# Down rows of two FFNs as pairs of seven half-width products, with part of their sums added by transfers

## The reference

```python
def swiglu(x, w_gu, w_down):
    g, u = jnp.split(x @ w_gu, 2, axis=-1)
    return (jax.nn.silu(g) * u) @ w_down
...
x = x + 0.5 * swiglu(rmsnorm(x, norm_ffn1_g[l]), ffn1_w_gu[l], ffn1_w_down[l])
...
x = x + 0.5 * swiglu(rmsnorm(x, norm_ffn2_g[l]), ffn2_w_gu[l], ffn2_w_down[l])
```

## Time and profile before

| | us |
|---|---|
| median of 3 runs | 1753.06 (1752.43 to 1754.81) |
| the profiled execution | 1753.69 |
| its span | 1751.5 |
| TensorE busy | 1745.0 (100%) |
| VectorE busy | 1180.3 (67%) |
| ScalarE busy | 847.4 (48%) |
| GpSimd busy | 135.4 (8%) |

### The profile page before, as it was taken

One profiled execution on the slowest core, in us unless ns is written; L12 is line 12 of the kernel. 1 busy time (PEld: TensorE's weight loads), 2 busy tenths in 40 slices (PEclk: granted clock), 3 DMA queues, 4 the chain that ended last, 5 costly groups with the idle time before them and its releaser, 6 DMA issues.

```text
span 1751.5 us, 26596 instructions
## 1 busy us (share of the span) xinstructions
PE 1745.0 (100%) x10407; PEld 1535.1 (88%) x10407; DVE 1180.3 (67%) x1843; ACT 847.4 (48%) x1442; POOL 135.4 (8%) x150
## 2 busy tenths in 40 slices
PE   9999999999999999999999999999999999999998
PEld 7889989878888899988888998988877888989897
DVE  7848748666776546865784784876688677747474
ACT  6425526454333335743553562654655543727274
POOL 0001011000000001100010110100232000000000
PEclk9999999999999999999999999999999999999999
DMA  5356556332123457733355655634421235555552
GB/s 184 89 166 176 145 151 151 111 106 85 53 85 107 114 151 177 175 108 98 95 149 140 168 150 150 173 100 131 141 61 61 85 96 138 127 145 141 142 139 72
DMA packets 92618, 220.65 MB, mean 126 GB/s; under 512 B 10800, under 2 KB 12080, under 8 KB 92496
## 3 DMA queue, kind: packets, MB, share of 16 engines
q1 hardware_dynamic: 74640, 186.29, 34.2%
q0 software_dynamic: 16576, 30.60, 10.8%
q10 hardware_dynamic: 1280, 2.08, 0.3%
HBM read 214.74 MB, written 2.10 MB: 124 GB/s over the span
## 4 chain that ended last, share of the span: by engine, by line
PE 97%; DVE 1%; ACT 0%; issue 0%; DMA 0%; DVEq 0%; ACTq 0%; POOLq 0%
PE ps L2083 19%; PE ps L2085 19%; PE ps L2084 19%; PE ps L2175 10%; PE ps L2177 10%; PE ps L2176 10%; PE ps L2105 2%; PE ps L2107 2%; PE ps L2106 2%; PE ps L2324 0%; PE ps L2454 0%; PE ps L2479 0%; PE ps L2465 0%; PE ps L2327 0%; PE ps L2312 0%
## 5 line engine op out<-in xcount | busy, mean ns | idle before, releaser
L2083 PE MATMUL ps<-Ahi,wh 128*128 128x512 f32 x913 | 357.1, 391 | 0.0
L2084 PE MATMUL ps<-Alo,wh 128*128 128x512 f32 x913 | 355.3, 389 | 0.0
L2085 PE MATMUL ps<-Ahi,wl 128*128 128x512 f32 x913 | 355.3, 389 | 0.0
L2175 PE MATMUL ps<-BThi,wh 128*128 128x256 f32 x1232 | 340.5, 276 | 0.0
L2176 PE MATMUL ps<-BTlo,wh 128*128 128x256 f32 x1232 | 340.4, 276 | 0.0
L2177 PE MATMUL ps<-BThi,wl 128*128 128x256 f32 x1232 | 340.4, 276 | 0.0
L571 ACT ACTIVATE wh<-raw 128x1024 fp32r<-128x1024 f32 (+1 forms) x206 | 213.1, 1036 | 222.3 <-PE ps L2085 187.9
L1189 DVE TENSOR_TENSOR wl<-raw,wh 128x1024 fp32r<-128x1024 f32 (+1 forms) x206 | 250.2, 1215 | 64.7 <-ACT wh L571 62.7
L2176 PEld LDWEIGHTS ps<-BTlo,wh 128*128 128x128 f32 x1232 | 231.6, 188 | 0.0
L2175 PEld LDWEIGHTS ps<-BThi,wh 128*128 128x128 f32 x1232 | 231.3, 188 | 0.0
L2177 PEld LDWEIGHTS ps<-BThi,wl 128*128 128x128 f32 x1232 | 231.3, 188 | 0.0
(11 more groups left out here) (367 smaller groups left out, 2729.0 us busy)
## 6 DMA issues: line engine op xcount, KB each, us to landing
raw<-in_w_gu SPq DMA_DIRECT2D x96, 256.0 KB, 3.7
raw<-in_w_d SPq DMA_DIRECT2D x32, 512.0 KB, 3.6
raw<-in_w_dn SPq DMA_DIRECT2D x32, 512.0 KB, 3.9
raw<-in_w_gu SPq DMA_DIRECT2D x22, 512.0 KB, 3.6
raw<-in_w_up SPq DMA_DIRECT2D x36, 256.0 KB, 3.8
sa<-in_w_gu SPq DMA_DIRECT2D x32, 256.0 KB, 3.8
sa<-in_w_gu POOLq DMA_DIRECT2D x32, 256.0 KB, 4.9
sc<-in_w_gu SPq DMA_DIRECT2D x32, 256.0 KB, 3.9
```

The source lines that it names most:

```text
L2083: pe.matmul(ps, wh[:, c], hi[:, k, :], start=(k == 0), stop=False)
L2084: pe.matmul(ps, wh[:, c], lo[:, k, :], start=False, stop=False)
L2085: last = pe.matmul(ps, wl[:, c], hi[:, k, :], start=False, stop=(k == nb - 1))
L2175: pe.matmul(ps, whi[:, w], bhi, start=(new and kp == 0), stop=False, skip_group_check=not new)
```

## The change

In both FFNs of the first block, the down rows of the first two groups become pairs: `DQ` numbers them, four for each group. The third group's rows stay units.

- **Order** (`SEQ`): the up pair of the inner tile behind a group now stands ahead of the group's down pairs (ups to tile 8, four down pairs, ups 9 to 16, four down pairs, ups 17 to 21, eight down units).
- **Activations**: for inner tiles 0 to 15 the gated product is written straight into blocks of `BF` or a new `DF`, and `pair_a` and `a_lo` go. For every two inner tiles VectorE makes the sums (`t_sums`, three operations), ScalarE one copy of 128 × 1792 (`t_high`) and VectorE one subtraction of the same size (`t_low`) into seven operands `DThi`, `DTlo`, which lie over `Ahi`, `Alo`, `Hhi` and `Hlo`. In the pair stage these stand in the iteration after each odd inner tile (and, in FFN 1, `t_high` and `t_low` of tiles 4 and 5 in the first pair), in the unit stage in iterations 1 to 4.
- **Results**: four half-width operations of VectorE add half of a product to its quarter of `X` (`x_add`); they stand where `merge` and `product` stand in an up pair. ScalarE's three taps are scaled (`x_tap`) and kept in `TA[5]`, `TA[8]` and `TA[6]`; GpSimd's queue adds them to `X` by two accumulating transfers, 128 × 256 and 128 × 512 (`kept`).
- **GpSimd's queue**: `kept` of pair m-2 stands ahead of the two transfers of pair m.
- The rows of `w_d` lie in another order of inner tiles (even ones first) in memory; the scratch for GpSimd's descriptors is 4096 bytes in place of 8192.

```diff
+        ups(0, 9)
+        downs(0)
+        ups(9, 17)
+        downs(1)
+        ups(17, 22)
+        downs(2)
...
+        def kept(p):
+
+            k, q = UNITS[p][1], DQ[p]
+            pool.wait_ge(s["tp"], 3 * PAIR[p] + 3)
+            pool.wait_ge(s["ev"], EV0[p] + 3)
+            pool.dma_start(X[:, k + 1, RIGHT], TA[6][:, (LEFT, RIGHT)[q % 2]], accum_op=ALU.add).then_inc(s["dk"], 16)
+            pool.dma_start(X[:, k, :], TA[(5, 8)[q % 2]], accum_op=ALU.add).then_inc(s["dk"], 16)
+
         def added(pairs):
-            for p in pairs:
+            pairs = list(pairs)
+            for m, p in enumerate(pairs):
+                if m > 1 and pairs[m - 2] in DQ:
+                    kept(pairs[m - 2])
...
+            def t_high(g, kp):
+
+                act.wait_ge(s["ts"], 8 * f + 4 * g + kp + 1)
...
+                act.activation(DThi[kp][:, :, :], act_blocks(g, kp)[:, 0:NP, :], ACT.Copy).then_inc(s["th"], 1)
+
+            def x_tap(p, i):
...
+                if i == 0 and q > 1:
+                    act.wait_ge(s["dk"], 32 * q - 32)
+                act.wait_ge(s["pe"], PEN[p][c])
+                act.activation(dst, BK[BANK[p][b]][:, LEFT], ACT.Copy, scale=scale).then_inc(s["tp"], 1)
...
+                t(p, 1)
+                pair_next(v, 0)
+                t(p, 2)
+                if i == 0 and f == 0:
+                    t_high(0, 2)
+                elif last[0] == "up" and last[1] < 16 and last[1] % 2 == 1:
+                    t_high(last[1] // 8, last[1] % 8 // 2)
+                pair_next(v, 1)
...
+            def t_low(g, kp):
+                dve.wait_ge(s["th"], 8 * f + 4 * g + kp + 1)
+                dve.tensor_tensor(DTlo[kp][:, :, :], act_blocks(g, kp)[:, 0:NP, :], f32(DThi[kp][:, :, :]),
+                                  ALU.subtract).then_inc(s["tl"], 1)
+
+            def x_add(p, i):
+
+                k = UNITS[p][1]
+                if i == 0 and DQ[p] % 8 == 4 and k == 0:
+                    dve.wait_ge(s["dk"], 32 * DQ[p])
+                b, c, dst, scale = ((2, 3, X[:, k, LEFT], 0.5), (0, 4, X[:, k + 1, RIGHT], -0.5),
+                                    (1, 5, X[:, k, RIGHT], 0.5), (0, 6, X[:, k + 1, LEFT], -0.5))[i]
+                dve.wait_ge(s["pe"], PEN[p][c])
+                dve.scalar_tensor_tensor(out=dst, in0=BK[BANK[p][b]][:, LEFT], scalar=scale, in1=dst,
+                                         op0=ALU.mult, op1=ALU.add).then_inc(s["ev"], 1)
...
+                if last[0] == "up":
+                    product(last[2], last[1])
+                elif last[0] == "dn":
+                    x_add(last[2], 3)
+                pair_lo(p, 4)
...
+                if due:
+                    t_sums(*tile, 0)
+                pair_lo(p, 5)
+                if due:
+                    t_sums(*tile, 1)
+                pair_lo(p, 6)
+                if due:
+                    t_sums(*tile, 2)
+                if v in PAIR:
+                    pair_lo(v, 0)
+                    total(v, 0)
+                if kind == "up":
                     merge(p, 0, TA[2][:, LEFT])
+                else:
+                    x_add(p, 0)
...
+            product(UP[f, 21], 21)
+            dve.wait_ge(s["dk"], 256 * f + 256)
...
+            if p in DQ:
+                return DThi[kp][:, c, :], DTlo[kp][:, c, :]
...
+                    if p in DQ and c == 0 and UNITS[p][1] == 0:
+                        pe.wait_ge(s["tl"], 4 * (DQ[p] // 4) + kp + 1)
```

More of the change, by code:

```diff
@@ new lines, in ffn @@
+            for i, (kind, j, p) in enumerate(SEQ[f]):
+                v = p + 2
+                last = SEQ[f][i - 1] if i > 0 else (None, 0, 0)
+                t = tap if kind == "up" else x_tap
+                pair_hi(p, 4)
+                if kind == "up" and j > 16:
+                    pair_a(j - 1)
+                t(p, 0)
+                pair_hi(p, 5)
+                pair_hi(p, 6)
+                t(p, 1)
[7 more added lines that the diff above has]
+                if v in PAIR:
+                    pair_hi(v, 2)
+                    pair_hi(v, 3)
+                else:
+                    hi(v)
+                    hi(v + 1)
+                if kind == "up":
@@ new lines, in ffn @@
+            for j in range(JS[f]):
+                u = UP[f, j]
+                kp = j - JS[f] + 5
+                if f == 0 and j == 0:
+                    lo(3)
+                    lo(4)
+                    norm(1, 1, 5)
+                elif j == 0:
+                    lo(u + 2)
+                    sums_lo(5, SS[:, :], Ahi, Alo)
+                    norm(6, 3, u + 3)
+                times_r(u, TA[j % 2])
+                if kp > 0:
+                    low_blocks(2 * f, kp - 1)
+                elif kp == 0:
+                    normed(2 * f, kp)
+                if j in (2, 4):
+                    t_low(0, j // 2 - 1)
+                dve.wait_ge(s["silu"], f * FT + j + 1)
+                own.add(dve.tensor_tensor(TA[4 + j % 2], TA[2 + j % 2], R[:, :], ALU.mult))
+                if j == JS[f] - 1:
+                    total(u + 2, 0)
+                    pair_lo(u + 2, 2)
+                elif j > 0 and (f == 1 or j > 2):
+                    lo(u + 3)
+                if 0 < kp < 4:
+                    normed(2 * f, kp)
+                dve.wait_ge(s["pe"], PEN[u + 1])
+                tiles_free(j)
+                own.wait()
+                dve.tensor_tensor(halves(j), BK[BANK[u + 1]][:, :].rearrange("p (h t) -> p h t", h=2),
+                                  TA[4 + j % 2].rearrange("p (h t) -> p h t", h=2), ALU.mult).then_inc(s["ev"], 1)
+                if f == 0 and j < 3:
+                    lo(6 + j)
+                elif j < JS[f] - 2:
+                    lo(u + 4)
+                elif j == JS[f] - 2:
+                    pair_lo(u + 4, 0)
+                    pair_lo(u + 4, 1)
+                else:
+                    pair_lo(u + 2, 3)
+                if 0 <= kp < 4:
+                    sums_of_blocks(2 * f, kp)
+                if j % 2 == 1:
+                    for step in range(3):
+                        t_sums(0, j // 2, step)
+                if j == JS[f] - 1:
+                    total(u + 2, 1)
@@ L1415, in ffn @@
                     dve.wait_ge(s["ev"], EV0[p])
                     merge(p, 1, TA[1][:, RIGHT])
[L1417 to L1440 removed]
+                else:
+                    x_add(p, 1)
@@ new lines, in ffn @@
+                if i == 0 and f == 0:
+                    t_low(0, 2)
+                elif due:
+                    t_low(*tile)
+                if v in PAIR:
+                    pair_lo(v, 2)
+                else:
+                    lo(v)
+                if kind == "up":
+                    merge(p, 2, TA[2][:, RIGHT])
+                else:
+                    x_add(p, 2)
+                if v in PAIR:
+                    pair_lo(v, 3)
+                    total(v, 1)
+                else:
+                    lo(v + 1)
@@ new lines, in ffn @@
+            product(UP[f, 21], 21)
+            dve.wait_ge(s["dk"], 256 * f + 256)
+            for n in range(KT):
+                u = DN[f, 2] + n
+                if n == 0:
+                    a_lo(22 * f, 5, TA[4])
+                feed(u + 2)
+                dve.wait_ge(s["pe"], PEN[u])
+                dve.scalar_tensor_tensor(out=X[:, n, :], in0=BK[BANK[u]][:, :], scalar=0.5, in1=X[:, n, :],
+                                         op0=ALU.mult, op1=ALU.add).then_inc(s["ev"], 1)
+                if n > 0:
+                    sums(n - 1)
+                dve.wait_ge(s["ev"], EVN[u])
+                after(n)
@@ L2644, in _tiles, with _halves @@
     return np.ascontiguousarray(w.reshape(k // P, P, n // P, P).transpose(2, 1, 0, 3))
+def _halves(w, groups):
+    order = list(range(w.shape[2]))
+    for a, b in groups:
+        order[a:b] = list(range(a, b, 2)) + list(range(a + 1, b, 2))
+    return np.ascontiguousarray(w[:, :, order, :])
 def _wide(w):
```

370 lines of the change are left out of this document (165 added, 205 removed).

## The result

The changed kernel took 1800.49 us (median of 4 runs, 1797.34 to 1804.18) against 1752.86 for the kernel before (4 runs beside it): a ratio of 1.0271, 95% interval 1.0257 to 1.0285. The forecast was "slower", by 10 us; it is slower by 48, and the time lies above the range.

A forecast was written before the change was run, and what follows sets the result against it. The prediction took TensorE to bound the kernel, busy for the whole span. From 1753.7 us, −21.6 (TensorE) +2 (VectorE) +29.9 (loop through GpSimd's queue) gave 1764.0, against the median 1763.4; range 1757 to 1779.

The forecast's parts named there:

- the loop: GpSimd's queue: third `x_add` of pair m-2, kept transfers, `sa`, `total`, next third `x_add`; 7.5 us a group, +29.9 us.
- TensorE's part: In four groups, eight down rows at 43.5 us become four pairs at 9.52 each, 38.1: −21.6 us.
- VectorE's part: VectorE keeps up on average; lateness in heavy iterations and at the first down pair costs +2 us (0 to 8).
- about 1.3 and 0.6: Lateness in us in FFN 1, where two heavy iterations follow each other, then the first down pair.
- the unit stage ... nothing: `t_low` in unit iterations 2 and 4 fits, 10.8 us of VectorE in the 10.9 of two units: no cost.
- ScalarE's part: Copies and taps take 5.5 of 9.52 us a pair and two `t_high` are cheaper than four `pair_a`: no cost.
- Hand-overs: Some six passes between engines in one closed turn through GpSimd's queue, at 0.04 us each: 0.25 us.
- Issues: GpSimd issuing the two kept transfers ahead of `sa`, 0.86 us each: 1.7 us a turn.
- La: Time from issue to landing of `sa` behind two kept transfers: 6.6 us, ends 4.2 and 7.6.
- L: Length of one closed turn through GpSimd's queue and VectorE, 4.85 us plus the landing of `sa`: 11.45 us.
- Break-even: Point where waits through GpSimd's queue cost 19.6 us over four groups, with `sa` landing in 5.96 us.
- Rival A: In GpSimd's queue `sa` lands in time and the kernel is faster, 1733.5 us without a stall; chance 0.28.

The follow-up runs named there:

- the version without the loop: The changed kernel with both kept transfers of pair m-2 issued behind the two sum transfers of pair m, not ahead: 1751.54 us, 0.9991 of the kernel before.
- the 4.3 with nothing ahead: Median landing of `sa` in us in the changed kernel with only the kept transfers moved behind, their wait left ahead of `sa`: 1751.5 us.
- the tiny transfers: The changed kernel, same order and waits, with each kept transfer carrying 8 columns in place of 256 or 512: 1780.7 us, 1.0154 of the kernel before.

## Why the prediction was wrong

The sign and the place were right. Four things were wrong: the gain of TensorE was put too high, and the costs of VectorE, of the loop and of slower up pairs too low.

- **TensorE's part, −21.6.** The shape is that of the up pairs, the time is not: 10.08 us a down pair, not 9.52, so 16 × 0.56 = 9.0 us of the gain never came. The step that failed is "the matmuls have the shape of today's pairs", taken as "the same time". Moving operands and weights by 64 to 256 bytes showed that the place counts.
- **VectorE's part, +2 (0 to 8).** Measured 8.8 in the version without the loop, with the slower clock behind the wait of 2.6 us in FFN 2. Of the waits named in FFN 1 ("about 1.3 and 0.6") one is there, 1.1 us before product 7 of the second pair; the first down pair has none. The failed step is "the unit stage ... nothing": the sum of the amounts fits, but the last iteration holds `t_low` ahead of the sum for the first pair. It was moved, and 4.0 us came back. The rest stays; VectorE is busy for 20.9 of 23.2 us there, which may be why, and no run tested it.
- **ScalarE's part, 0.** Right as an amount; ScalarE only hands on the wait for `total`. SP's queue cost nothing either.
- **The loop, 4 × 7.5 = +29.9.** Measured 45.5. By its parts: VectorE 2.9 forecast, 2.90 measured. Hand-overs 0.25 forecast, 0.68 measured: 0.12 from the landing to `total`, but 0.56 from the end of `x_add` to GpSimd's queue; I had taken six at 0.04 between VectorE and ScalarE and none to GpSimd. Issues 2 × 0.86 = 1.7: the queue issues 0.54 apart (the row that I cited, four in 2.19 us, already has 0.55 each), but the durations grow by 0.36 each (0.87, 1.22, 1.58), so `sa` is through 2.65 us after the first starts where it would be through after 0.87 alone, 1.78 more. Of the landing of 7.90 from its start, 0.71 belong to that; what is left is **7.2 against La = 6.6**. The term in La that failed is the queueing behind the two kept transfers: I put at most 1.7 on a median of 4.9, with 1.7 read from two issues that stood 1.71 apart, which shows no rate of the queue; against the 4.3 with nothing ahead they add 2.9. Together L = 12.56, not 11.45: 16 × 1.11 = 17.8 us. Since twelve of the turns are measured against 10.08 and not 9.52, 6.7 fall off. That makes 29.9 + 17.8 − 6.7 = 41.0. Up to the start of product 7 of the up pair behind each group, where the last wait ends, the trace has 11.4, 10.0, 10.5 and 10.0, together 41.9. The other 3.6 are that product itself: 12 matmuls that take 1.36 us without the loop and 1.5, 2.7, 2.7 and 2.1 with it, in three of the groups at the half clock. The prediction had no term for the clock.
- **The rest.** More up pairs ran at 118 ns than before: 4.1 us in the version without the loop. The kernel before has such pairs too, at the start of FFN 2 (912.3 to 922.2 and 922.2 to 932.1, 9.89 us each at a full clock); the prediction took its period from FFN 1 alone. Behind the loop's groups, the up pairs from the second on lose 5.2 us more, about 3.4 by the half clock that goes on into the second one and 1.8 by more pairs at 118. Nothing in the prediction spoke of that.

The sum: −21.6 + 9.0 + 8.8 + 4.1 = +0.3 for the version without the loop (spans: −0.2), then + 45.5 + 5.2, less 0.9 for FFN 2's first pair, whose wait has no half clock behind it in the changed kernel: +50.1 (spans: 49.6). Break-even stands wrong too: even with no loss in the loop this change is worth 0.1% at most (0.9991, interval 0.9982 to 1.0001), not 1.1%.

Rival A asked whether `sa` lands in time. In the changed order it does not; with the kept transfers behind it does, and still the time is 1751.5 and not rival A's 1733.5, for the first two reasons of the list and the slower up pairs. The Trainium skill's fit for GpSimd's DMAs (DMA: Bandwidth & Descriptors, Anatomy of one DMA — SWDGE (gpsimd) path), 2.0 us plus the bytes over 436 GB/s, gives an estimate of 2.0 us for the tiny transfers, which landed in 2.3 to 3.8, and of 2.6 us for `sa`, which took 4.0 to 4.7 with nothing ahead of it. Neither agrees, and the second is further off.

Of what the profile was to show, these were right: `sa` issued 11.0 us after the start of pair m-2 (106.55 to 117.52; 11.5 expected), `total` idle for it, TensorE waiting for `x_add`. Down pairs took 10.1 to 14.3 us (first of a group: 10.1, without a wait), where 11 to 12 were expected. Landings of 7.1 to 8.7 us lay above the 6 to 7.5.

## What to carry to other kernels

A wait put at the head of a queue costs nothing until something behind it feeds what it waits for. Then compare one turn (hand-over + issues + landing + the work on the way) with the time that the pipeline gives it, one period or two; only what is over is lost. Issue what the next step needs first and what only drains last: the same transfers, the same wait, 49 us apart. On an engine with little slack, ask of each long operation when its result is due, not whether the sum of the work fits; and before pricing new matmuls like old ones, look at where their operands lie.
